# Mix projection of a decoder layer on one core: six contraction steps by seven block products in place of eight

## What is computed

```python
    g = jax.nn.sigmoid(gates.astype(jnp.float32)).astype(x.dtype).reshape(Bsz, S, 3, D_MODEL)
    merged = g[:, :, 0] * (o_a @ w_a) + g[:, :, 1] * (o_b @ w_b) + g[:, :, 2] * (o_c @ w_c)
    return merged @ w_out
...
        x = layer_norm(ALPHA * x + h, ln1_g[l], ln1_b[l])
        h = memory_cross_attention(x, mem, w_xq[l], w_xkv[l], w_xo[l])
```

## Time and profile before

| | |
|---|---|
| time, median of 3 runs | 873.6 us (873.24 to 873.79) |
| the profiled execution | 873.84 us, of which its span is 872.1 us |
| TensorE busy | 861.3 us of the span, 99% |
| VectorE, ScalarE, GpSimd busy | 553.1, 372.4 and 81.2 us |
| granted TensorE clock | 0.999 of full speed |
| last gate round ends, mix product starts | 420.97 us into the span |

### The profile page before, as it was taken

The page is one execution under the profiler, slowest core; times in us unless marked ns, Lnnn a source line. Parts: engine busy times, 40 slices in busy tenths (PEclk is TensorE's granted clock), DMA queues, the critical chain, the costliest instruction groups (busy, mean ns, idle before and its releaser), DMA issues.

```text
span 872.1 us, 13309 instructions
## 1 busy us (share of the span) xinstructions
PE 861.3 (99%) x5143; PEld 747.3 (86%) x5143; DVE 553.1 (63%) x1016; ACT 372.4 (43%) x747; POOL 81.2 (9%) x103
## 2 busy tenths in 40 slices
PE   9999999999999999999999999999999999999996
PEld 8988888877678888888889979899999999888785
DVE  4344347769632626262767579679888888877934
ACT  4112157229642222222324554355656556434511
POOL 3100000081310000000000000011111111000000
PEclk9999999999999999999999999999999999999999
DMA  8534530430003333236531311313332333751101
GB/s 289 165 97 132 134 98 25 145 93 6 1 2 97 97 97 96 96 96 235 190 105 66 129 49 49 97 49 110 127 104 97 98 97 105 266 210 48 49 25 72
DMA packets 71832, 90.36 MB, mean 104 GB/s; under 512 B 3149, under 2 KB 62359, under 8 KB 71775
## 3 DMA queue, kind: packets, MB, share of 16 engines
q1 hardware_dynamic: 71391, 89.15, 31.3%
q0 software_dynamic: 384, 0.43, 0.3%
HBM read 87.05 MB, written 2.52 MB: 103 GB/s over the span
## 4 chain that ended last, share of the span: by engine, by line
PE 94%; DVE 3%; issue 1%; DMA 1%; ACT 1%; SPq 0%; DVEq 0%; POOLq 0%; POOL 0%; ACTq 0%
PE ps L2400 19%; PE ps L2402 19%; PE ps L2401 19%; PE ps L2970 7%; PE ps L2972 7%; PE ps L2971 7%; PE ps L2565 3%; PE ps L2642 3%; PE ps L2602 3%; PE ps L3028 1%; PE ps L3029 1%; PE ps L3030 1%; PE ps L2437 1%; DMA x_nat<-in_x 1%; PE ps L3073 1%
## 5 line engine op out<-in xcount | busy, mean ns | idle before, releaser
L2400 PE MATMUL ps<-xt_hi,w_hi 128*128 128x512 f32 (+1 forms) x400 | 155.6, 389 | 0.3 <-DVE w_lo L2110 0.3
L2402 PE MATMUL ps<-xt_lo,w_hi 128*128 128x512 f32 (+1 forms) x400 | 154.8, 387 | 0.0
L2401 PE MATMUL ps<-xt_hi,w_lo 128*128 128x512 f32 (+1 forms) x400 | 154.8, 387 | 0.0
L1138 ACT CAST w_hi<-raw 128x1024 fp32r<-128x1024 f32 (+1 forms) x49 | 50.5, 1035 | 133.3 <-PE ps L2402 121.6
L1901 DVE TENSOR_TENSOR w_lo<-raw,w_hi 128x1024 fp32r<-128x1024 f32 x30 | 36.7, 1224 | 90.1 <-ACT w_hi L1305 90.1
L2400 PEld LDWEIGHTS ps<-xt_hi,w_hi 128*128 128x128 f32 x400 | 75.1, 188 | 16.1 <-issue 1.1
L2402 PEld LDWEIGHTS ps<-xt_lo,w_hi 128*128 128x128 f32 x400 | 75.1, 188 | 15.4
L2401 PEld LDWEIGHTS ps<-xt_hi,w_lo 128*128 128x128 f32 x400 | 75.1, 188 | 15.1
L1592 DVE TENSOR_TENSOR w_lo<-raw,w_hi 128x1024 fp32r<-128x1024 f32 (+1 forms) x49 | 59.1, 1207 | 39.1 <-ACT w_hi L1138 38.9
L2971 PE MATMUL ps<-xt_hi,w_lo 128*128 128x256 f32 x288 | 81.5, 283 | 0.0
L2972 PE MATMUL ps<-xt_lo,w_hi 128*128 128x256 f32 x288 | 81.5, 283 | 0.0
(11 more groups left out here) (391 smaller groups left out, 1979.1 us busy)
## 6 DMA issues: line engine op xcount, KB each, us to landing
raw<-in_w_in SPq DMA_DIRECT2D x24, 1024.0 KB, 5.0
raw<-in_w_ffn_in SPq DMA_DIRECT2D x36, 512.0 KB, 4.4
raw<-in_w_ffn_out SPq DMA_DIRECT2D x7, 1024.0 KB, 4.8
raw<-in_w_mix_out SPq DMA_DIRECT2D x4, 1024.0 KB, 4.9
raw<-in_w_ffn_in SPq DMA_DIRECT2D x4, 1024.0 KB, 5.3
out_w<-in_w_ffn_out SPq DMA_DIRECT2D x4, 1024.0 KB, 8.8
raw<-in_w_branch_b SPq DMA_DIRECT2D x4, 512.0 KB, 3.9
resid<-in_x SPq DMA_DIRECT2D x1, 2048.0 KB, 9.5
```

The source lines that it names most:

```text
L1138: act.copy(hi, src).then_inc(hi_done, 1)
L2400: pe.matmul(dst, a_hi, b_hi, start=start, stop=False, skip_group_check=reopened)
L2401: pe.matmul(dst, a_lo, b_hi, start=False, stop=False, skip_group_check=reopened)
L2402: return pe.matmul(dst, a_hi, b_lo, start=False, stop=stop, skip_group_check=reopened)
```

## The change

The product is done in blocks: rows 0 to 255 and 256 to 511, contraction steps 0, 2, 4 and 1, 3, 5, columns 0 to 511 and 512 to 1023. Seven products of three steps (`N_MIX`) take the place of eight; contraction steps 6 and 7 stay plain, row tile by row tile. For that,

- VectorE forms four sums of the left blocks (`m_sums`) in the last gate round, twelve operations of 128x768 with the rests, and ScalarE casts them (`m_round`); the last round is written out on its own, and its gate products are kept in `sg` and added up later (`add_gated`, `split_gated`), between the rests of the mix weights;
- the mix weights of steps 0 to 5 come as four quarters (`mix_quarter`, 0.75 MB each) into buffers of their own; VectorE forms three sums of them, four with the one made over (`MIX_T1`, `T2`, `T3` and `T2` again, which the text calls T4), each 128x1536; hi parts and rests are made in pieces of 128x512, 21 of them (`mix_round`, `mix_rest`), in four half slots, so a piece can be made only when the product step four before it is over with;
- ScalarE copies PSUM banks on as starting values (`mix_seeds`, `mix_second_seeds`), and VectorE takes two products away into `resid` (`keep_scaled`) before their banks are used again, so that `resid` must have been loaded by then;
- P4, which only row tiles 2 and 3 need, stands behind row tiles 0 and 1; the transposes stand after it, and that of tile 2 now between the two memory-key pieces;
- rests of `k` and `c` weights move into the gap of a layer norm.

```diff
+N_MIX = 3
+def mix_op(kind, k):
+    return N_MIX * OUT_PRODUCTS.index(kind) + k
...
+            sp.wait_ge(m_sum_lo, 4)
+            mix_quarter(MIX_B12, 0, 1).then_inc(mix_in, 16)
+            mix_quarter(MIX_B11, 0, 0).then_inc(mix_in, 16)
+            sp.wait_ge(piece_done, (N_PAIR - 1) * 8 + PG + 6)
+            mix_quarter(MIX_B22, 1, 1).then_inc(mix_in2, 16)
+            mix_quarter(MIX_B21, 1, 0).then_inc(mix_in2, 16)
             for c in range(CM, CF):
+                if c == CM + 1:
+                    sp.wait_ge(mix_lo, mix_op("P1", N_MIX))
+                    sp.wait_ge(mix_t, 3)
+                    sp.dma_start(resid[:, :, :], A["x"][0].rearrange("(t p) n -> p t n", p=P)).then_inc(resid_in, 16)
+                    sp.wait_ge(mix_lo, mix_op("P5", N_MIX))
                 load(c)
...
+                if c == CM + 1:
+                    sp.wait_ge(mix_prod, mix_op("P7", N_MIX))
                     for i, w in enumerate(("ln1_g", "ln1_b")):
                         sp.dma_start(gb[:, i, :], A[w][0:1, :].to_broadcast([P, D])).then_inc(gb_in, 16)
...
+            def mix_round(kind, k):
+                m = mix_op(kind, k)
...
+                if m < 4:
+                    act.wait_ge(piece_done, PM - 1 + m // 2)
+                else:
+                    act.wait_ge(mix_prod, m - 3)
+                act.copy(out_slot(m, 0), MIX_RIGHT[kind][:, k, :]).then_inc(mix_hi, 1)
...
+            def mix_rest(kind, k):
+                m = mix_op(kind, k)
+                dve.wait_ge(mix_hi, m + 1)
+                dve.tensor_tensor(out_slot(m, 1), MIX_RIGHT[kind][:, k, :], f32(out_slot(m, 0)), ALU.subtract).then_inc(mix_lo, 1)
...
+            for k in range(N_MIX):
+                mix_rest("P5", k)
+            dve.tensor_tensor(MIX_T3, MIX_B22, MIX_B12, ALU.subtract).then_inc(mix_t, 1)
+            for k in range(N_MIX):
+                mix_rest("P6", k)
...
             norm_sums(0)
-            norm_out(0)
+            norm_gamma(0)
+            rest_of(PKX)
+            norm_end(0)
             norm_sums(1)
-            norm_out(1)
+            norm_gamma(1)
+            rest_of(PKX + 1)
+            norm_end(1)
             turn_tile(1, 0)
             norm_sums(2)
             norm_out(2)
             turn_tile(1, 1)
-            norm_sums(3, (0,))
+            norm_sums(3)
+            norm_gamma(3)
+            rest_of(PXQ)
+            norm_end(3)
             turn_tile(1, 2)
-            norm_sums(3, (1,))
-            norm_out(3)
-            rest_of(PXQ)
...
-            rows_tail(PM, KT, N_TAIL, 0, m_hi, m_lo, lambda k: pe.wait_ge(merge_step, 6 * (k + 1)))
-            rows_tail(PM, KT, N_TAIL, 1, m_hi, m_lo)
+            for kind in OUT_PRODUCTS[:-1]:
+                mix_product(kind)
+            mixed = PM - 2 * N_MIX
...
+            rows_tail(mixed, KT, KT - 2 * N_MIX, 1, m_hi, m_lo)
+            mix_product(OUT_PRODUCTS[-1])
             turn_tile(1, 0)
-            rows_tail(PM, KT, N_TAIL, 2, m_hi, m_lo)
+            rows_tail(mixed, KT, KT - 2 * N_MIX, 2, m_hi, m_lo)
             turn_tile(1, 1)
...
+            rows_tail(mixed, KT, KT - 2 * N_MIX, 3, m_hi, m_lo)
...
+                if n == 0:
+                    turn_tile(1, 2)
             turn_tile(1, 3)
```

More of the change, by code:

```diff
@@ L118 @@
 PM = 63
[L119 to L123, removed]
+PKX = 65
+PXQ = 67
+PVX = 69
+PXO = 71
+PF = 73
 PO = PF + 2 * (D_FF // P)
@@ L647, in split_slot @@
         def split_slot(p):
-            for first, n, hi, lo in ((PM + 2, 4, x_hi, x_lo), (PKX, 2, k_hi, k_lo), (PXQ, 2, c_hi, c_lo), (PXO + 1, 1, k_hi, k_lo)):
+            if PM <= p < PKX:
+                return x_hi[:, p - PM + 2, :], x_lo[:, p - PM + 2, :]
+            for first, n, hi, lo in ((PKX, 2, k_hi, k_lo), (PXQ, 2, c_hi, c_lo), (PXO + 1, 1, k_hi, k_lo)):
                 if first <= p < first + n:
@@ L743, in h_left, with m_left @@
             return {"P5": (g1_hi, g1_lo), "P7": (g3_hi, g3_lo)}[kind][part][:, :, :]
+        def m_left(kind, part):
+            m = (m_hi, m_lo)[part]
+            if kind == "P1":
+                return m[:, 0:2 * N_MIX:2, LO]
+            if kind == "P2":
+                return m[:, 1:2 * N_MIX:2, LO]
+            if kind == "P4":
+                return m[:, 1:2 * N_MIX:2, HI]
+            if kind == "P3":
+                return m[:, 0:2 * N_MIX:2, HI]
+            return {"P5": (n1_hi, n1_lo), "P6": (n2_hi, n2_lo), "P7": (n3_hi, n3_lo)}[kind][part][:, :, :]
+        MIX_T1 = raw[0][:, 0:N_MIX * 512].rearrange("p (k c) -> p k c", k=N_MIX)
+        MIX_B11, MIX_B12 = mix_b[:, 0, :, :], mix_b[:, 1, :, :]
+        MIX_B22, MIX_B21, MIX_T2, MIX_T3 = (mix_w[:, i, :, :] for i in range(4))
+        MIX_RIGHT = {"P1": MIX_B11, "P2": MIX_B21, "P3": MIX_B22, "P5": MIX_T1, "P6": MIX_T2, "P7": MIX_T3, "P4": MIX_T2}
         def out_t(n, k):
@@ L1904, in _, with gate_iteration @@
             MERGE_STEPS = 6
-            def gate_iteration(i, last):
+            def gate_iteration(i):
                 for q in range(8):
@@ new lines, in _ @@
+            m_add(M_B, "P2")
+            dve.wait_ge(m_whole, 4)
+            dve.wait_ge(m_sum, 3)
+            dve.tensor_tensor(M_B, M_B, M_A, ALU.subtract).then_inc(m_sum, 1)
+            gate_rest(LAST_I, 4, 0)
+            for kind in ("P5", "P7", "P6", "P3"):
+                m_rest(kind)
+            gate_rest(LAST_I, 5, 0)
+            gate_rest(LAST_I, 6, 0)
+            dve.wait_ge(mix_in, 32)
+            dve.wait_ge(lo_done, 8 * LAST_I + PG + 6)
+            dve.tensor_tensor(MIX_T1, MIX_B12, MIX_B11, ALU.subtract).then_inc(mix_t, 1)
@@ new lines, in _, with keep_scaled @@
+            dve.tensor_tensor(MIX_T2, MIX_B21, MIX_T2, ALU.subtract).then_inc(mix_t, 1)
+            mix_rest("P7", 0)
+            rest_of(PM)
+            mix_rest("P7", 1)
+            split_gated(1)
+            mix_rest("P7", 2)
+            dve.wait_ge(resid_in, 16)
+            dve.wait_ge(mix_prod, mix_op("P5", N_MIX))
+            def keep_scaled(t, bank):
+                v = resid[:, t, 512:1024]
+                dve.scalar_tensor_tensor(out=v, in0=v, scalar=ALPHA, in1=ps[:, bank, :], op0=ALU.mult,
+                                         op1=ALU.add).then_inc(mix_kept, 1)
@@ L1946, in norm_sums @@
+            for r in range(2):
+                keep_scaled(r, 5 + 2 * r)
+            mix_rest("P3", 0)
+            rest_of(PM + 1)
+            mix_rest("P3", 1)
+            mix_rest("P3", 2)
+            dve.wait_ge(mix_prod, mix_op("P7", N_MIX))
+            for r in range(2):
+                keep_scaled(2 + r, 4 + 2 * r)
+            for k in range(N_MIX):
+                mix_rest("P4", k)
             def norm_sums(n, halves=(0, 1)):
```

222 lines of the change are left out of this document (173 added, 49 removed).

## The result

The changed kernel takes **877.75 us**, median of 5 runs (876.87 to 878.28), against 873.79 for the kernel before in the same round (873.24 to 875.25): ratio 1.0041, 95% interval 1.0027 to 1.0056. It is slower by 0.4%; the forecast was 873.0 with a range of 871.0 to 875.6. The profiled execution took 878.04 us and has a span of 876.3 us.

A forecast was written before the change was run, and what follows sets the result against it. TensorE was taken as the bound (94% of the chain); of 4.08 us of matmuls removed, VectorE's lists in mix and norm left 0.65 gained at the query: 873.84 - 0.65 = 873.19, on the median's footing 873.0, range 871.0 to 875.6.

The forecast's parts named there:

- the part on the norm: First layer norm after the mix: over 2 us lost to VectorE's list, the query starting at 473.64.
- the rule on the drain: Skill's rule that VectorE's next operation waits for an empty pipe; by it 878.1, set aside for starts 0.60 apart.
- it waits 1.8 us: TensorE, ready for the norm's last transposes at 470.6, waits for tile 3's last step, seen at 472.4.
- the marker: Start of the query projection, 474.29 before; behind it both kernels do the same work in the same order.
- The last gate round: Twelve 128x768 operations added, 3.6 us per gap against 4.21 idle on VectorE: nothing lost.
- the transfers: Weight quarters, resid and the norm's gain and bias all land before they are wanted: nothing lost.
- The mix: Mix product: 1.55 us lost to VectorE's list, plus a 0.15 tail; step 6 starts at 447.15.
- Rival 3: Slower: VectorE's lists in mix and norm run at full operation lengths, 878.1; 13%.
- Rivals 1: The mix list doesn't bind, P7 and P3 don't wait, the norm list starts 1.7 earlier; 871.3; 12%.
- 2: TensorE stays the bound everywhere, 869.7; needs the two VectorE lists 1.7 and 2.1 us shorter; 5%.
- 4: The norm's gain and bias land late, 10 us after issue, giving 874.8; 7%.
- 0.65 of 4.08: Net gain at the query, 0.65 us, of the 4.08 us that 18 fewer matmuls take off TensorE.

The follow-up runs named there:

- Experiment 2: Changed kernel with tile 3's gap filled by tile 2's two xt_lo (one operand in PSUM), c_lo after the last step; 877.11 us, ratio 1.0040.
- 5: Changed kernel with one k_lo moved from row tile 0's gap to ahead of the first sum, where VectorE idled; 876.61 us, ratio 1.0031.
- 10: Kernel before, with only c_lo of piece PXQ put into row tile 3's gap between gamma step and last step; 873.68 us, ratio 1.0000.
- 1: Changed kernel with k_lo of tiles 0 and 1 and c_lo of tile 3 moved ahead of the gamma step; 877.15 us, ratio 1.0040.
- experiment 4: Changed kernel with 21 unread 128x256 matmuls added in TensorE's wait ahead of the last transposes; 876.29 us, ratio 1.0028.
- 6: Changed kernel with k_lo halves ahead of gamma steps, xt_lo in gaps of tiles 2 and 3, c_lo after the last step, MIX_T4 late; 873.81 us, 1.0000.
- 9: As 6, plus 24 query matmuls ahead of the last transposes, and memory-key and first query hand-overs ahead of tile 3's xt_lo; 873.10 us, 0.9991.
- experiment 3: Changed kernel with MIX_T4 (128x1536 on VectorE) moved from ahead of P7's rests to behind P3's; 877.64 us, ratio 1.0046.

## Why the prediction was wrong

**The step that failed** is in the part on the norm: "Where k_lo or c_lo now fills that gap, 1.0 + 1.20 + 1.14 decides, 3.37 with the hand-over." It took the gap as idle time of VectorE into which 1.14 us fit, and GpSimd's share in it, which the sentence before names, as unmoved. The runs show that GpSimd's `rstd` does not get done while VectorE runs the operation beside which it was issued, if that has both tensors in SBUF. It ends 0.40 to 0.45 after that operation, so the last step comes 4.17, 4.04 and 4.03 after the second sum in tiles 0, 1 and 3, 2.1 us more in all. Experiment 2 tells this from a busy VectorE, 5 from a GpSimd that had long been idle, 10 from everything else in the change, and 1 shows that the gamma step does it as well.

The Trainium skill has this (SBUF — State Buffer, SBUF: two separate sides): VectorE and GpSimd share a port pair; between a VectorE operation with two SBUF inputs and a GpSimd operation that reads SBUF, the one that starts first has it for its whole length, and the other fully blocks. `rstd` reads `var` and `half` from SBUF, and the traces agree, with 0.40 to 0.45 us from the end of the one to the end of the other; no row here shows the reverse, a VectorE operation held up by GpSimd. Of the Trainium skill I had weighed the rule on the drain, and not this one.

The row was there to be read, too. The four roots of the first norm in the trace of before last 0.55 to 0.58, and I took those. The view of that one line gives 547, 550 and 1527 ns as its shortest, median and longest. The long one, on GpSimd, and what VectorE ran then:

```profile
515.88 1.53 POOL L1112 TENSOR_TENSOR rstd<-var,half 128x1 f32<-128x1 f32 x1 [2.42 <-ACT var L1324]
```

```profile
515.72 1.28 DVE L1986 SCALAR_TENSOR_TENSOR norm_part<-resid,neg_mean,gb 128x1024 f32<-128x1024 f32 x1
```

A second one there, of 1.15, tells something more:

```profile
528.46 1.15 POOL L1112 TENSOR_TENSOR rstd<-var,half 128x1 f32<-128x1 f32 x1 [2.36 <-ACT var L1324]
```

```profile
527.98 1.22 DVE L1592 TENSOR_TENSOR c_lo<-raw,c_hi 128x1024 fp32r<-128x1024 f32 x1
529.12 1.28 DVE L1986 SCALAR_TENSOR_TENSOR norm_part<-resid,neg_mean,gb 128x1024 f32<-128x1024 f32 x1
```

It ends at 529.61, 0.41 behind the end of `c_lo`, although a gamma step with its tensors in SBUF follows without a pause. So here the operation under way when `rstd` was issued held it, and the next one did not (the changed kernel has the same pair of rows at 531.95).

**The second step** that failed is TensorE's "it waits 1.8 us", priced at its length alone, and with it the marker: from the query on, both kernels were taken to need the same time. It waited 0.99 and 2.79, and the clock fell to half behind the longer one: 1.6 us more, shown by experiment 4. Such a wait can have a price behind it. At 0.6 to 1.0 us (experiments 6 and 9) there was none. I named no rival for it. (The marker itself was reckoned at 474.29 from the scores; the query's row in the kernel before is at 474.11. The same 10.05 us stood behind it in both kernels, so the sum does not change.)

**What was right.** The last gate round and the transfers cost nothing; resid, the gain and bias, and the quarters end no wait of VectorE in this stretch. The mix lost 1.9 us where 1.7 were forecast, 1.3 of it by four waits of TensorE at P7's and P3's steps (0.17 to 0.30 each, and 0.11 behind each), 0.4 at P1's third step, where 0.2 was laid out; experiment 3 took 1.0 of it away by moving one sum in VectorE's list behind the rests that TensorE waited for. The query started as soon as the `xt_lo` of tile 2 were through (their end 475.65, the query 475.70), as laid out, 2.5 us later than said. The starts of neighbouring operations were 0.60 and 1.14 apart as taken.

**The sum with what was measured:** 873.0, and 2.1 for the hold-up, 0.2 for the mix, 0.2 for hand-overs, 1.6 for the clock makes 877.1. The mix starts 0.4 earlier than before, and 1.1 are lost behind the scores, nearly all in the two places named above: 877.8, where the median is 877.75.

**The rivals.** Rival 3 gave 878.1, close to the time, and was wrong: its mechanism, operations at their full lengths, did not occur (in the changed trace rests of 128x512 start at 441.65 and, two of them, at 443.38; what follows starts at 442.25 and 444.59, 0.60 and 1.21 later). Rivals 1, 2 and 4 did not occur either. That the forecast's own gain was small (0.65 of 4.08) should have told me how little it took to turn its sign.

## What to carry to other kernels

A gap in an engine's timeline is not free for every instruction: before filling one, look at who works in it, and whether the filler slows just that one; here halves ahead of the gamma step or an operand in PSUM fitted, and a 128x1024 rest with both tensors in SBUF cost 0.8 us. For an operation on which a chain hangs read its shortest and its longest duration, not the usual one, and look at what ran beside the longest. When a change takes matmuls away from a TensorE that was always busy, the first thing it makes is a pause, and the pause may cost the clock as well as its own length; the engine that fed it was never tested at the new pace.

## What the runs showed of the hardware that I had not expected

- A GpSimd operation on 128x1 that takes 0.55 us by itself ends 0.40 to 0.45 us after the VectorE operation beside which it was issued, if that has both tensors in SBUF (`TENSOR_TENSOR` and `SCALAR_TENSOR_TENSOR` of 128x1024 alike), and takes 0.55 beside one with an operand in PSUM (experiment 2). A second such operation right behind the first did not hold it again (529.61 in the kernel before).
- 21 unread matmuls in a pause of TensorE made the kernel 1.46 us faster.
- After a pause of 2.3 to 2.8 us the granted clock was 0.50 in the profiles of the changed kernel and of experiments 1, 2, 3 and 5: for the transposes themselves in 1 and 5 (1.94 and 1.97 us for 1.09), only from the query on in the changed kernel. In the profiled execution of experiment 5 a gain of 0.8 ahead of the pause was gone behind it; the median kept it.
